# Norm roots, norm weights and sums of squares of a first transformer block: where they stand among the projections

## What is computed

```python
def rms_norm(x, g):
    xf = x.astype(jnp.float32)
    y = xf * lax.rsqrt(jnp.mean(xf * xf, axis=-1, keepdims=True) + EPS)
    return (y * g.astype(jnp.float32)).astype(x.dtype)
...
def swiglu_ffn(u, w_gate_up, w_down):
    g, up = jnp.split(u @ w_gate_up, 2, axis=-1)
    return (jax.nn.silu(g) * up) @ w_down
...
    for i in range(DEPTH):
        kind, j = i % N_MIXERS, i // N_MIXERS
        u = rms_norm(h, mix_pre_g[i])
        if kind == 0:
            y = dilated_attention_mixer(u, a_w_in[j], a_w_out[j], cos, sin)
        elif kind == 1:
            y = differential_attention_mixer(u, b_w_in[j], b_w_out[j], b_lam_q1[j], b_lam_k1[j],
                                             b_lam_q2[j], b_lam_k2[j], b_sub_g[j], cos, sin, i)
...
        h = h + rms_norm(y, mix_post_g[i])
        u = rms_norm(h, mem_pre_g[i])
        y = memory_cross_attention(u, rms_norm(mem, mem_kv_g[i]), x_wq[i], x_wkv[i], x_wo[i])
        h = h + rms_norm(y, mem_post_g[i])
        u = rms_norm(h, ffn_pre_g[i])
        y = swiglu_ffn(u, w_gate_up[i], w_down[i])
        h = h + rms_norm(y, ffn_post_g[i])
```

## Time and profile before

| what | us |
|---|---|
| median of 3 runs | 2538.22 (2530.23 to 2540.72) |
| the profiled execution, as timed | 2545.15 |
| its span | 2543.3 |
| mean granted clock of TensorE | 0.886 |
| TensorE busy | 2095.4 (82%) |
| DVE, ScalarE, GpSimd busy | 982.9, 710.7, 672.3 |

### The profile page before, as it was taken

The page is one execution under the profiler, slowest core; times in us unless marked ns, Lnnn a source line. Parts: engine busy times, 40 slices in busy tenths (PEclk is TensorE's granted clock), DMA queues, the critical chain, the costliest instruction groups (busy, mean ns, idle before and its releaser), DMA issues.

```text
span 2543.3 us, 35461 instructions
## 1 busy us (share of the span) xinstructions
PE 2095.4 (82%) x14027; PEld 1646.4 (65%) x14027; DVE 982.9 (39%) x1825; ACT 710.7 (28%) x1074; POOL 672.3 (26%) x224
## 2 busy tenths in 40 slices
PE   3979787997977779997999986577889999668855
PEld 2958777996957769996768763233467686534423
DVE  4361525523275434603745343111256543321212
ACT  3344342343353333332222212112223122112211
POOL 2624444884715525870002000000000020000000
PEclk8989898998978889998998887788989988779977
DMA  4413333553504324536310137999223102377793
GB/s 146 150 50 117 105 111 100 186 179 107 165 31 130 116 67 150 178 121 201 131 42 27 42 124 291 421 399 391 86 103 133 66 1 100 124 306 291 301 421 154
DMA packets 202119, 404.52 MB, mean 159 GB/s; under 512 B 18483, under 2 KB 152006, under 8 KB 177270
## 3 DMA queue, kind: packets, MB, share of 16 engines
q1 hardware_dynamic: 198230, 388.85, 41.7%
q0 software_dynamic: 3744, 13.63, 1.4%
HBM read 399.18 MB, written 3.28 MB: 158 GB/s over the span
## 4 chain that ended last, share of the span: by engine, by line
PE 70%; DVE 11%; DMA 9%; DVEq 4%; ACT 2%; issue 2%; SPq 1%; ACTq 1%; POOL 0%; POOLq 0%
PE ps L874 9%; PE ps L875 9%; PE ps L876 9%; PE ps L1086 9%; PE ps L1393 7%; DMA weight_ring<-in_w 5%; DMA acts<-in_w 4%; DVEq L1868 3%; PE ps L1313 2%; PE ps L1415 2%; PE ps L914 2%; PE ps L904 2%; PE ps L1102 2%; DVE acts L1883 1%; PE ps L1168 1%
## 5 line engine op out<-in xcount | busy, mean ns | idle before, releaser
L1825 POOL TENSOR_TENSOR weight_ring<-weight_ring 128x2048 fp32r<-128x2048 f32 x132 | 603.8, 4586 | 528.6 <-ACT weight_ring L1481 528.6
L874 PE MATMUL ps<-weight_ring 128*128 128x256 f32 x1824 | 535.4, 294 | 75.1 <-DVE acts L1883 71.9
L876 PE MATMUL ps<-weight_ring 128*128 128x256 f32 x1568 | 446.5, 285 | 0.0
L875 PE MATMUL ps<-acts,weight_ring 128*128 128x256 f32 x1472 | 423.8, 288 | 0.0
L874 PEld LDWEIGHTS ps<-weight_ring 128*128 128x128 f32 x1824 | 353.4, 194 | 87.5 <-issue 55.5
L876 PEld LDWEIGHTS ps<-weight_ring 128*128 128x128 f32 x1568 | 306.8, 196 | 0.0
L875 PEld LDWEIGHTS ps<-acts,weight_ring 128*128 128x128 f32 x1472 | 287.1, 195 | 3.1 <-issue 3.1
L1393 PE MATMUL ps<-weight_ring,x_g 128*32 128x512 f32 x1056 | 187.2, 653 | 94.9 <-DMA acts<-in_w 57.5
L1481 ACT ACTIVATE weight_ring<-weight_ring 128x2048 fp32r<-128x2048 f32 x132 | 247.0, 1888 | 64.3 <-PE ps L876 48.4
L1086 PE MATMUL ps<-acts,weight_ring 128*128 128x272 f32 x896 | 219.0, 406 | 5.0 <-ACTq L1688 5.0
L1086 PEld LDWEIGHTS ps<-acts,weight_ring 128*128 128x128 f32 x896 | 176.2, 197 | 44.6 <-issue 6.8
(11 more groups left out here) (421 smaller groups left out, 3784.3 us busy)
## 6 DMA issues: line engine op xcount, KB each, us to landing
weight_ring<-in_w SPq DMA_DIRECT2D x132, 1024.0 KB, 23.2
weight_ring<-in_w_gate_up SPq DMA_DIRECT2D x44, 1024.0 KB, 5.1
acts<-in_w SPq DMA_DIRECT2D x40, 1024.0 KB, 26.5
weight_ring<-in_w_in SPq DMA_DIRECT2D x16, 2048.0 KB, 8.7
h_area<-in_w SPq DMA_DIRECT2D x20, 1024.0 KB, 28.1
weight_ring<-in_x_wkv SPq DMA_DIRECT2D x16, 1024.0 KB, 5.3
weight_ring<-in_w_down SPq DMA_DIRECT2D x16, 1024.0 KB, 5.2
weight_ring<-in_a_w_in SPq DMA_DIRECT2D x12, 1024.0 KB, 6.8
```

The costliest lines, as they stand in the source:

```text
L874: nc.tensor.matmul(o, wh, xh, start=start, stop=False)
L875: nc.tensor.matmul(o, wh, xr, start=False, stop=False)
L876: return nc.tensor.matmul(o, wr, xh, start=False, stop=stop)
L1825: nc.gpsimd.tensor_tensor(r12(w), w, r12(high[:, n % HIGH, 0:k * 256]).bitcast(F32), ALU.subtract).then_inc(rest_ready, 1)
```

## The change

It touches the first block alone.
- Input norms: the projection takes h times the norm weight, without the reciprocal root. `pre_norm` is gone; ScalarE writes the high part (`high_of_h`) and DVE the remainder (`rest_of_h`), the first as soon as a pair of slices of h is complete. The reciprocal is applied behind the projection: on the rotation tables (`rope_u`), on the values at their eviction by token (`rstd_tok`, got by two transposes), on the memory queries and on the gate tiles, which DVE now evicts, with Silu in place behind it. The up tile is left unscaled; the down branch's norm takes that up with a row of eps (`eps_u`) added by a one-row matmul in front of its sum (`sum_branch`).
- The sum for an input norm stands behind the first projection that it serves (for the feed-forward behind the first pair; for the queries before `mv` 3, as it did). `late_norm` makes the reciprocal.
- Branch norms: the norm weight goes into the eviction (two copies with a scale), squares come first, and the sum is spread in four groups among the projections. `post_norm` scales and adds in quarters.
- The memory queries read `oT`, `oH`. The root of the mixer's branch norm stands behind the eviction of `mv` 0.

```diff
             for g in range(4):
                 take("o", l, g)
+                if g == 1:
+                    take("norm", n0 + 1)
...
+            def sum_branch(n, base, g, eps_row=False):
+                b = begin("norm", n) if g == 0 else tiles[("norm", n)][0]
+                if eps_row and g == 0:
+                    nc.tensor.matmul(ps[:, b, 0:S1], ones[0:1, :], eps_u[0:1, :], start=True, stop=False)
+                pe.wait_ge(post_sq, base + g + 1)
+                for k in (2 * g, 2 * g + 1):
+                    last = nc.tensor.matmul(ps[:, b, 0:S1], ones[:, :], sq[:, k, 0:S1],
+                                            start=(k == 0 and not eps_row), stop=(k == KT - 1))
+                if g == 3:
+                    last.then_inc(full[b], 1)
...
                 for g in range(4):
                     project(("o", l, g), o_src)
-                sum_squares(n0 + 1, post_sq, 4 * (3 * l), 4, S1)
+                    if g:
+                        sum_branch(n0 + 1, 12 * l, g - 1)
                 for c in range(4):
                     if c == 3:
                         sum_squares(n0 + 2, pre_sq, 2 * (p0 + 1), 2, S1)
                     project_values(("mv", l, c))
+                    if c == 0:
+                        sum_branch(n0 + 1, 12 * l, 3)
-                src = u_tiles(p0)
+                src = u_tiles(p0, o_src)
...
-                sum_squares(n0 + 3, post_sq, 4 * (3 * l + 1), 4, S1)
-                sum_squares(n0 + 4, pre_sq, 2 * (p0 + 2), 2, S1)
-                src = u_tiles(p0 + 1)
+                    if g:
+                        sum_branch(n0 + 3, 12 * l + 4, g - 1)
+                sum_branch(n0 + 3, 12 * l + 4, 3)
+                src = u_tiles(p0 + 1, u_of)
                 for c in range(11):
                     project(("g", l, c), src)
                     project(("u", l, c), src)
+                    if c == 0:
+                        sum_squares(n0 + 4, pre_sq, 2 * (p0 + 2), 2, S1)
...
+            def high_of_h(col, arrived, dst):
+                for k in range(KT):
+                    if arrived is not None and k % 2 == 0:
+                        act.wait_ge(h_ready, arrived + k // 2 + 1)
+                    ins = nc.scalar.activation(r12(dst[:, k, :]), hx[:, k, :], ACT.Copy, scale=gains[:, col + k:col + k + 1])
+                    if k % 2:
+                        ins.then_inc(uh_ready, 1)
...
-                    nc.scalar.activation(yT[:, 2 * g:2 * g + 2, 0:S1], y, ACT.Copy)
                     nc.scalar.activation(sq[:, 2 * g:2 * g + 2, 0:S1], y, ACT.Square).then_inc(post_sq, 1)
+                    for a in range(2):
+                        nc.scalar.activation(yT[:, 2 * g + a, 0:S1], y[:, a, :], ACT.Copy,
+                                             scale=gains[:, col + 2 * g + a:col + 2 * g + a + 1])
...
+            def rest_of_h(p, col, q, dst, dst_h):
+                dve.wait_ge(uh_ready, 4 * p + q + 1)
+                for k in (2 * q, 2 * q + 1):
+                    ins = nc.vector.scalar_tensor_tensor(out=r12(dst[:, k, 0:S1]), in0=hx[:, k, :], scalar=gains[:, col + k:col + k + 1],
+                                                         in1=r12(dst_h[:, k, :]).bitcast(F32), op0=ALU.mult, op1=ALU.subtract)
+                ins.then_inc(u_ready, 1)
+            def late_norm(n):
+                dve.wait_ge(std_ready, n + 1)
+                nc.vector.reciprocal(rstd_u[:, :], std[:, 0:S1])
+                nc.vector.scalar_tensor_tensor(out=eps_u[:, :], in0=std[:, 0:S1], scalar=DM * 1e-6, in1=std[:, 0:S1],
+                                               op0=ALU.mult, op1=ALU.mult)
+                nc.vector.drain().then_inc(late_ready, 1)
...
+                for q in range(4):
+                    two = slice(2 * q, 2 * q + 2)
+                    if q < 3:
+                        scaled(q + 1)
                     settle()
+                    nc.vector.tensor_tensor(hx[:, two, :], hx[:, two, :], yT[:, two, 0:S1], ALU.add).then_inc(h_ready, 1)
+                    if rest is not None and q > 0:
+                        rest_of_h(*rest[0:2], q - 1, *rest[2:])
```

177 lines of the change are left out of this document (111 added, 66 removed).

## The result

The changed kernel takes 2482.6 us (median of four runs, 2474.6 to 2484.97), the kernel before, run beside it, 2538.14; the ratio is 0.978, 95% interval 0.976 to 0.980. The forecast was 2484.

What follows compares the result with a forecast made beforehand. TensorE was taken to set the first block's pace except at the norms. Gains of 66.0 us less losses of 11.8, 54 net, from the median 2538.2 gave 2484 us, range 2470 to 2497, chance 0.62.

Steps and rivals of the forecast that it cites:

- start: Program start: root, reciprocal and scaling leave the front, first chunk ready at 45.5; 65.9 against 75.74, 9.8 us gained.
- mixer to queries, with attention: Mixer output to memory queries: T+58.7 against 72.8, 14.1 us gained a layer; value evictions and transposes cost a little.
- second output to feed-forward: Second output projection to feed-forward: 26.4 against 35.85 us, 9.4 gained a layer, 18.8 in two.
- layer change, from the later end on: Layer change: 32.9 against 42.15 us, 9.2 gained, after counting 2.25 for the last projection's later end.
- feed-forward, with the later end: Feed-forward: gate multiply makes GpSimd late, 3.7 us a layer, taken as 8 for both; last projection ends 2.25 later.
- end of the block, behind its last projection: End of first block: last projection ends 2.25 us later, norm behind it stays hidden behind the DMAs; 2.25 lost.
- T': New end of the last projection before a norm, 1.8 us later than T; the memory queries end at T'+56.9.
- the wait for squares: Before the sums of the memory queries' norm: TensorE waits from 18.75 to 23.1, 4.4 us where 3.71 stands now.
- Clock: After TensorE's waits: clock returns late, from 297.97 to 308.65 in the earlier trace; slow matmuls take some 0.21 us.
- rival B: Five restarts: clock stays up or returns sooner, 4.5 us each, no feed-forward loss; 31 us more gained, 2453; chance 0.13.
- the chain of lateness: Feed-forward cycles: lateness 0.75, 2.85, 4.95 us, then starts over; 1.05 us lost every third cycle.
- Rival C: Feed-forward: closed loop whose lateness never starts over, cycles of 13.2 to 17 us; up to 130 us, 2614; chance 0.04.

Runs made afterwards that it cites:

- halves: Changed kernel with the residual addition and the split of h done by halves instead of quarters: 2473.5 us, ratio 0.973 to the kernel before.
- table ahead: Changed kernel with a constant's root queued on ScalarE before each branch norm's last tile work, so the root's table loads early: 2476.7 us, 0.972.
- the run with the early root: Changed kernel with the mixer branch's last sums, root, split of h and squares ahead of the first value tile: 2466.8 us, 0.970.
- the two runs without the ring: Changed kernel without the gate tile's multiply (part of the computation left out), 2454.8 us; changed kernel with weight splits before Silu, 2472.5 us.
- sums whole: Changed kernel with branch-norm sums behind the second output and feed-forward all after the last projection tile instead of spread: 2472.0 us, 0.972.
- splits ahead of Silu: Changed kernel with ScalarE copying the weights' high parts in the feed-forward before it waits for the gate multiply and takes Silu: 2472.5 us, 0.974.

## Why the prediction was right, and where its terms were off

| term | predicted gain | measured | what was off |
|---|---|---|---|
| start | 9.8 | 12.0 | clock back 4.0 us behind the restart |
| mixer to queries, with attention | 13.4 a layer | 12.9, 11.7 | sums 6.7 us, not 5.0 |
| second output to feed-forward | 9.4 a layer | 11.5 (layer 0) | clock back after 8.4, not 10.7 us |
| layer change, from the later end on | 11.5 | 14.4 | clock back after 6.2 us |
| feed-forward, with the later end | -6.3 (layer 0) | -6.7 | 3.36 us of waits against 3.7 |
| end of the block, behind its last projection | 0 | 0.1 | |

- **The total**: the terms add up to 54 us, and the block lost 60.6. That the forecast of 2484 lies 1.4 us from the measured 2482.6 is in part luck: the terms are 6.6 us low, and the medians differ by 5.1 us less than the traced blocks.
- **Idle time**: right to tenths. T' to the first feed-forward matmul was priced at 9.7 us and is 9.6, with the wait of 7.66; the wait for squares 4.4 and is 4.18. Undoing the deferral brings the old gaps back.
- **Clock**: the step that failed in size. I carried the 10.7 us of the earlier trace rows to every restart. The real ones were 4.0, 6.2 and 8.4 us; a clock that is back 2.3 to 6.7 us sooner is worth half of that, 1.2 to 3.3 us a place, so rival B's mechanism held in part. What sets the length is open, as the halves and the table ahead show. Behind the mixer it went the other way: the sums ran at the low clock and took 6.7 us instead of 5.0.
- **Mixer to queries**: the order was priced rightly. The sum, T'+56.9 plus 0.75 of small terms and the 0.7 up to the first score, is 58.35, and 59.05 in the trace (243.61 to 302.66). The run with the early root shows that 7.3 us a layer of this stretch come from the root's place behind value 0, a cost that I had in the sum (the wait of 4.4, the slow sums) without naming it as the change's weak point.
- **Start**: TensorE began at 47.12, not 45.5, as the memory's sums ran at the low clock in this execution, so that their root came 1.5 us later than before the change; the sooner clock outweighed it.
- **Feed-forward**: the chain of lateness, the third cycle and six waits all showed. I had 3.7 us a layer and rounded both up to 8; the waits are 6.7, and 7.9 came back in the stretches when they went.
- **Rival C**: it needed the lateness never to start over. It does so in the third cycle, where GpSimd's gap lets the cast (0.43 us) and subtraction (0.69) through, and the two runs without the ring put its whole cost at 8 us.
- **Slips that change little**: the 35.85 us of the earlier trace rows end 0.2 us ahead of the eviction at 410.44. The uncertainties as listed add up to 2471.5 to 2500.5, not 2470 to 2497. Every third of 11 cycles at 1.05 us is 3.9, not 3.7. Rival C's cycle reaches 17.8 us, not 17.
- **What carries the gain**: by undoing, the feed-forward's deferral about 15 us of the block, that of the first projections 10, the queries' buffer 13 in its two stretches (11 of the block), the weights at the evictions 0 to 1.5, quarters none, spread sums minus 8. These do not add up to 60.6, and need not, since parts undone one at a time share waits and the clock's return, as sums and table did; the rest (remainders of h made without a cast of DVE's, the queries' reciprocal applied behind, the shorter start) was not undone and stays open in its split.

## What to carry to other kernels

Take roots and reciprocals out of the path in front of a projection; where the weights are nearly as late, as at this start, it bought 1.9 us. Look where a deferred step is queued on the engine that also feeds the weights: two of the change's own orders (root behind value 0, splits behind Silu) cost 14.7 and 8 us. Pipelining the input of a stalled TensorE in finer pieces can be worth nothing: here it started 2.1 us sooner and the clock came back later. Before adding up small gains, ask whether two of them shorten the same wait.

## What the runs showed of the hardware

- The granted clock came back from 0.50 (1.2 GHz) to 1.00 at 4.0, 6.2 and 8.4 us behind the restarts of the changed kernel and, before the change, 10.7. Where no matmul waited, it was 4.0 (start) and 5.3 (halves); with waits of 0.45 us between pairs 5.7 (table ahead), 5.9 (sums whole), 6.2 and 8.4. So such waits alone do not tell it.
- A restart somewhat sooner brought what follows sooner by twice as much: counted from the first score, 0.95 us at the restart were 2.17 at the next norm's sums (table ahead), 1.07 us were 2.21 (sums whole).
- DVE's cast of 512 columns, a single input in SBUF, took 0.43 us alone and 4.91 beside GpSimd's subtraction, ending 0.3 us behind it. The page "SBUF — State Buffer" of the Trainium skill (Who interferes with whom) names casts among the operations that can take the pair of ports shared with GpSimd and lets the later one wait for the whole instruction. The prediction, which drew on the same section for instructions with a single SBUF input, left that exception out. The trace of the kernel with the splits ahead of Silu agrees with it (GpSimd's subtractions end at 429.90 there):

```profile
425.27 4.91 DVE L1948 CAST probs<-qkv 128x512 fp32r<-128x512 f32 x1 [0.17 <-issue]
430.26 0.69 DVE L1950 TENSOR_TENSOR qkv<-qkv,probs 128x512 fp32r<-128x512 f32 x1
```
- Eight remainders of 256 columns took 3.25 us where GpSimd's subtraction began at their end, 8.77 where it ran at their start and again in their midst, and 11.78 where it ran from their midst on.
